# New priority constants and assumed landing times in the planner of a streaming encoder kernel on 8 cores

## What is computed

```
z = x @ w_in                                  # 1024 -> 2560, split in u, v, gb, gc, xin
v = layernorm per head(v);  a = u * (w_s (128x128, masked) @ v + b_s)
b = gb * causal_conv3(gc * xin)
x = LN(ALPHA*x + concat(a, b) @ w_out)
q = x @ w_q; p = softmax(q k^T / 16); x = LN(ALPHA*x + (p v) @ w_mem_o)      # 256 memory tokens
x = LN(ALPHA*x + (silu(x @ w_gate) * (x @ w_up)) @ w_down)                   # 1024 -> 2816 -> 1024
```

## Time and profile before

| | |
|---|---|
| time, median of 3 runs | 3340.69 us (3310.32 to 3353.55) |
| the profiled execution's own time | 3351.93 us |
| its span on the slowest core (core 7) | 3350.4 us |
| spans of the eight cores | 3272.5 to 3350.4 us |
| granted TensorE clock by core | 0.975 to 0.984 |
| DMA | 620.69 MB, mean 185 GB/s |

### The profile page before, as it was taken

The page is one execution under the profiler, slowest core; times in us unless marked ns, Lnnn a source line. Parts: engine busy times, 40 slices in busy tenths (PEclk is TensorE's granted clock), DMA queues, the critical chain, the costliest instruction groups (busy, mean ns, idle before and its releaser), DMA issues.

```text
span 3350.4 us, 54366 instructions; the slowest of 8 cores (3272.5 to 3350.4 us)
## 1 busy us (share of the span) xinstructions
PE 3139.9 (94%) x17604; PEld 1660.0 (50%) x17604; DVE 2181.0 (65%) x4244; ACT 1062.8 (32%) x2012; POOL 383.5 (11%) x356
## 2 busy tenths in 40 slices
PE   8999899999999998899988999799996998979998
PEld 3544444554645454354543545455463553635554
DVE  5774256677767675666756767486683866748664
ACT  4362215242423324133241332323231242323421
POOL 2111011101011000111001011010110101101010
PEclk9999999999999999899998999899998999989999
DMA  9879999675877969767697677956779679786762
GB/s 189 163 160 200 183 258 227 208 193 178 209 179 229 170 209 146 159 214 177 198 149 165 201 189 223 158 178 197 179 229 123 211 188 152 220 135 209 188 181 87
DMA packets 292614, 620.69 MB, mean 185 GB/s; under 512 B 178992, under 2 KB 179120, under 8 KB 262128
## 3 DMA queue, kind: packets, MB, share of 16 engines
q1 hardware_dynamic: 113632, 498.02, 47.8%
q10 hardware_dynamic: 166464, 44.06, 15.5%
q0 software_dynamic: 12240, 75.13, 13.4%
HBM read 582.27 MB, written 64.89 MB: 193 GB/s over the span
## 4 chain that ended last, share of the span: by engine, by line
PE 78%; DMA 17%; issue 2%; DVE 1%; ACT 1%; POOL 0%; ACTq 0%; SPq 0%; DVEq 0%; POOLq 0%
PE bank L91 78%; DMA rb<-wsc 9%; DMA rb<-w_pieces 3%; DMA ra<-wsc 2%; DMA F<-xb 1%; DMA ra<-w_pieces 1%; DMA wsc<-rb 0%; POOL rs L723 0%; DMA xbuf<-x_prompt 0%; DVE rb L659 0%; DMA y_prompt<-xbuf 0%; DVE bank L91 0%; DVE xin L879 0%; DMA WTS<-w_s_t_s 0%; DVE xbuf L754 0%
## 5 line engine op out<-in xcount | busy, mean ns | idle before, releaser
L91 PE MATMUL bank<-F,rb 128*128 128x512 f16 (+2 forms) x5024 | 920.9, 335 | 11.2 <-DMA rb<-wsc 7.5
L91 PE MATMUL bank<-ra,F 128*128 128x512 bf16 x3424 | 797.3, 383 | 29.0 <-DMA ra<-wsc 22.8
L91 PE MATMUL bank<-rb,hT 128*128 128x512 bf16 (+1 forms) x2744 | 639.5, 391 | 110.4 <-DMA rb<-wsc 104.6
L91 PEld LDWEIGHTS bank<-F,rb 128*128 128x128 f16 (+1 forms) x5024 | 489.7, 98 | 372.2 <-issue 15.1
L723 POOL TENSOR_TENSOR rs<-ve,mhalf 128x1 f32<-128x1 f32 (+1 forms) x260 | 334.9, 1291 | 2179.3 <-DVE ve L721 2079.8
L91 PEld LDWEIGHTS bank<-ra,F 128*128 128x128 bf16 x3424 | 335.4, 98 | 399.4 <-issue 43.8
L91 DVE SCALAR_TENSOR_TENSOR xbuf<-xbuf,bank 128x512 f32<-128x512 f32 x384 | 258.6, 678 | 400.5 <-PE bank L91 383.0
L91 PEld LDWEIGHTS bank<-rb,hT 128*128 128x128 bf16 (+1 forms) x2744 | 273.6, 100 | 455.0 <-issue 157.9
L91 PE MATMUL bank<-F,ra 128*128 128x512 bf16 x1920 | 434.2, 382 | 14.2 <-DMA ra<-w_pieces 8.5
L91 PE MATMUL bank<-early,rb 128*128 128x256 f16 (+2 forms) x3104 | 362.1, 262 | 16.3 <-DVE bank L91 9.1
L775 ACT ACTIVATE xb<-xbuf 128x1024 bf16<-128x1024 f32 (+1 forms) x128 | 135.2, 1057 | 630.2 <-DVE mv L749 339.7
(11 more groups left out here) (119 smaller groups left out, 1841.6 us busy)
## 6 DMA issues: line engine op xcount, KB each, us to landing
rb<-wsc SPq DMA_DIRECT2D x455, 512.0 KB, 5.9
ra<-wsc SPq DMA_DIRECT2D x149, 1024.0 KB, 6.0
rb<-w_pieces POOLq DMA_DIRECT2D x34, 1024.0 KB, 14.3
y_prompt<-xbuf SPq DMA_DIRECT2D x60, 512.0 KB, 4.9
xbuf<-x_prompt SPq DMA_DIRECT2D x14, 2048.0 KB, 10.4
wsc<-rb SPq DMA_DIRECT2D x16, 1024.0 KB, 10.5
F<-x_prompt_t POOLq DMA_DIRECT2D x14, 1024.0 KB, 18.6
ra<-w_pieces POOLq DMA_DIRECT2D x13, 1024.0 KB, 17.2
```

Of the source, the lines that this page charges most:

```text
L91: return f(*[r(x) for x in a], **{n: r(x) for n, x in k.items()})
```

## The change

Only constants change. In the planner's table of late landings the transposes go from 10 to 9.0 us, xt from 14 to 12.7, ra loads from 4 to 5.4, and rb loads, which had none, get 3.5. In part A the four combined pieces get one priority, the first output halves change a little, the four attends stand 0.088 apart and not 0.050, and the second output halves get 0.732 and 0.749 and not 0.860 and 0.877, so they rank ahead of all but the first attend. In part B (from tile 1 on) the gate and up pieces are spread over 0.325 and not 0.400, and the down pieces start at 1.494 and not 1.644, each step about as long as before.

```diff
--- before.py
+++ after.py
@@ -135,7 +135,7 @@
 
     LAT = 0.20
     LAT_TO_PE = 0.45
-    LATE = {"tr": 10, "xt": 14, "rA": 4}
+    LATE = {"tr": 9.0, "xt": 12.7, "rA": 5.4, "rB": 3.5}
     DEPTH = 3 << 20
 
     def __init__(self, nc, banks, pools):
@@ -1194,7 +1194,7 @@
             for c in tiles:
                 in_proj_v(c, rg, brg)
             for m in range(4):
-                at(0.183 + 0.001 * m)
+                at(0.183 + 0.000 * m)
                 rg, brg = piece("A", "in_c%d" % m, t)
                 for c in tiles:
                     in_proj_c(c, m, rg, brg)
@@ -1202,18 +1202,18 @@
                 op("sync", lambda e: e.dma_start(out=cvp_o, in_=halo_p[:].rearrange("p m r -> p (m r)")),
                    [buf("halo_p%d" % m) for m in range(4)] + [buf("halo_p")], [], dma="o_cp", nbytes=1 << 12)
             for half in range(2):
-                at(0.480 + 0.086 * half)
+                at(0.483 + 0.070 * half)
                 rg, brg = piece("A", "out%d" % half, t)
                 for c in tiles:
                     out_half(c, half, rg, brg, 0)
             at(0.657)
             pieces = [piece("A", "m%d" % hp, t) for hp in range(2)]
             for s in range(4):
-                at(0.657 + 0.050 * s)
+                at(0.657 + 0.088 * s)
                 for c in tiles:
                     attend(c, s, pieces)
             for half in range(2):
-                at(0.860 + 0.017 * half)
+                at(0.732 + 0.017 * half)
                 for c in tiles:
                     out_half(c, half, *piece("A", "n%d" % half, t), 1)
 
@@ -1326,7 +1326,7 @@
         def run_B(tiles, t):
             n = NF // 2
             for j in range(n):
-                S.prio = t + 1.0 + 0.400 * j / n if t else 0.892 + 0.600 * j / n
+                S.prio = t + 1.0 + 0.325 * j / n if t else 0.892 + 0.600 * j / n
                 if j == 7:
                     pinned.clear()
                 if t == T_SEVEN and j == 0:
@@ -1346,7 +1346,7 @@
                 return
             for half in range(2):
                 for kp in range(3):
-                    S.prio = t + 1.644 + 0.142 * half + 0.081 * kp
+                    S.prio = t + 1.494 + 0.168 * half + 0.083 * kp
                     rg, brg = piece("B", "d%d_%d" % (half, kp), t)
                     for c in tiles:
                         down(c, half, kp, rg, brg)
```

## The result

The changed kernel takes **0.956 of the time before, 95% interval 0.942 to 0.970**: faster. Applied to the median before, that is 0.9561 x 3340.69 = 3194 us. Its own executions are 3171.2 (the profiled one) and 3206.4; two more, in which the cores of one die show a lower granted clock (3343.9 and 3737.7), are left out of every comparison here, as are such executions of the other kernels.

The account below looks back on a forecast made before the run. It took TensorE on core 7, its work plus idle time and the clock lost after it, as the bound. 3350.4 - 157.2 - 24.6 + 63 = 3232 us, 11 less on the median's scale: 3221, stated as 3225, range 3175 to 3325.

Parts of the forecast that it names:

- The bound and the cause: Core 7: TensorE busy 94% of 3350.4 us; a just-started transpose ahead of xt slows all transfers for about 40 us.
- The first rival: Even passes: long flights of xt stay although block 2's transpose starts earlier; 3287 us, no change by the measure, chance 0.25.
- The attends: Part A: wider spacing moves block 2's transpose from 2.1 us ahead of xt to some 8 to 10 in pass 8.
- The sum, core 7: Whole kernel on core 7: 3350.4 - 157.2 - 24.6 + 63 = 3232 us.
- The ten passes: Core 7, passes 4 to 13, each from one xt issue to the next: 187.25 us each, -157.2 in all.
- the tail: Core 7, from the last xt to the end: 398.7 us falls to core 2's undisturbed 374.1, -24.6.
- The +63: Core 7: waits that stay or are new, from loads landing late, VectorE and a long xt, +63 us together.
- Late landings: Loads landing late in the passes: 3 us a pass, times 12, 36 us.
- One long xt: One long flight of xt left on the slowest core: 20 us at most, taken at 15.
- VectorE: After the last attend, FFN layer norms meet other VectorE work: backlog 11.7 us, cost 1 a pass, 12 in all.
- The cover: Around xt: matmuls before first use of loads beside it cover 28.9 or 21.7 us, so a 15.8 us flight everywhere.
- The ring loads in gate-up: Gate-up: rb loads with under 10 us of matmuls between release and first use fall from 46 to 5; waits shrink.

Follow-up runs that it names:

- e12: The kernel before, with attend block 2's DMA transpose held until just behind the transposed-input load (xt) in even passes 4 to 14: 3213.9 and 3217.5 us.
- e5: The changed kernel, with xt and the 1 MB ra load waiting for the VectorE operation that releases block 3's transpose, all leaving within 1 us: 3380.2 us.
- e9: The kernel before with the change's table of late landings alone, all priorities old: ratio 1.003.
- e10: The changed kernel without the new 3.5 us landing of rb loads: ratio 0.970.
- e8: The kernel before with all priorities of the change but the old table of late landings: ratio 0.976.
- e6: The kernel before with only the attends spread 0.088 apart instead of 0.050: ratio 0.965.
- e7: The kernel before with only part B's constants of the change (gate, up and down pieces): 3248.6 us.
- e11: The kernel before with the new table of late landings and the attends 0.088 apart, other priorities old: ratio 0.977.

## Why the prediction was right

It said 3225 us, 3175 to 3325, faster with 0.62; the measurement gives 3194, a ratio of 0.956. Step by step:

*The bound and the cause.* The reading of the earlier trace rows, that a transpose which has just started when xt and a 1 MB piece arrive slows every transfer of the core, was called "my reading and not shown". For xt and the rb loads at its side it is shown now, from both sides: e12 takes the arrangement away in the kernel before, and the long flights and the beat go; e5 puts it into the changed kernel, and the long flights come back. "Every transfer" was too much: the ra load of e5 took 11.9 us where xt took 38.5. The first rival (the order of the two does not matter, 0.25) is refuted by the same runs. It was also where a rule of the Trainium skill led (DMA: Bandwidth & Descriptors, "Queues, rings and completion order": a DMA engine takes its queues in turn). Taking turns may well be what the engines do, but it says nothing about which came first, and in e12 and e5 that is what changes: the instructions and their order on each engine are those of their parents. A little else moves with it: in e12 block 3's transpose goes out 2.8 us later in pass 8, and in e5 xt and the ra load leave some 3 us later, nearer to the transposes behind them. But pass 8 of e5 has none near behind, and xt took 38.5. What in the DMA engines makes the order count stays open.

*The attends.* Block 2's transpose was to move in pass 8 to 8 to 10 us ahead of xt: 9.7. In the other passes it was to be 4 to 6; it is 6.8 to 9.9. Block 3's was to stay "about 7 us behind xt"; it is 2.4 to 3.2. That miss did no harm, and this is luck: the count of the order could not tell it, and e5, with block 3's 0.7 ahead, 3.4 us from there, is slower than before.

*The sum, core 7.* The ten passes were to give -157.2 and gave 1859.7 - 2029.7 = -170.0; the tail -24.6, and 364.9 - 398.7 = -33.8; the stretch up to pass 4, taken as unchanged, +4.4. So the two terms that go were 22 too small: the undisturbed passes of before that I took as the floor, 188.4 and 186.1, still held a little waiting (188.40 with 187.29 busy in the first line of the earlier trace rows). The +63 that were to come back were the mis-sized part. *Late landings*, 3 us a pass, 36 in all: TensorE idles for 0.5 us in ten passes. *One long xt*, 15: there is none in 96. *VectorE*, 12: TensorE's waits for it on the line of the earlier trace rows fell from 9.1 to 3.8 us on the slowest core. Its work in the 50 us from xt is 39.1 us, not 45 to 48, against 33.4 before; that TensorE's eight banks cover what queues up, as the prediction argued, fits this and was not tested. Together -170.0 - 33.8 + 4.4 = -199, and 3350.4 - 199.4 = 3151.0, core 7's span. The slowest core is another one now, at 3169.6, since the cores differ by 19 us after. So for core 7 the sum was 81 too high (3232 against 3151.0). That the forecast of 3225 lies only 31 from 3194 is partly luck: the slowest core is 19 above core 7, and the second execution took 35 more than the profiled one.

*The cover.* The worked-out 28.9 and 21.7 us of matmuls were never needed, as the longest flight is 15.1. Cover without the cure is worth little: e9 had longer leads and 44 long flights, and gained nothing.

*The ring loads in gate-up* got no term of their own, and that was a gap. Their assumed landing is worth nothing with the old priorities and, by the distance of e10 (0.970) from the change (0.956), about 1% with the new; the intervals overlap (0.964 to 0.976, 0.942 to 0.970), so the size is not settled. That the wait it removes is real is seen in e8's timeline.

*The signs to look for.* Passes of 184 to 188 on core 7 (to 189.4 on all), xt of 10 to 15, rb waits of 3.5, a clock of 0.99: all as said or better.

## What to carry to other kernels

If an even-odd beat or a spread between cores shows up in passes of equal instructions, list the long transfers and what was issued in the 3 us ahead of each; a load that leaves while a DMA transpose has just started is the suspect. Let the transpose land first or send it behind, and check this by the issue times of a trace, since counts of matmuls in the planned order misled in four runs here (e6, e7, e9, e11). Follow a wait that is put down to VectorE one step further: at L659 it was a load.

## What the runs showed of the hardware

A DMA transpose is 3.1 us alone. Issued at xt or up to 3.3 us behind it, it takes 11 to 23 us and xt 12 to 16 (the middle 80% of 558 such, medians 15.8 and 13.4). Issued 0.3 to 2.45 us ahead of xt, it takes 4 to 39, median 26, and xt 12 to 36, median 21. What is lost is bandwidth. Two stretches of the kernel before, core 7, in the slow flight and in the next pass's good one, where a transpose is under way too; the last two numbers are the DMA share and GB/s:

```profile
1748.00:1760.00 12.00, 1.79 (x9) 0.59 (x6) 0.00 (x0) 1.06 (x1) 0.00 (x0) 0.68 0.94 40
...
1947.60:1963.40 15.80, 15.80 (x75) 7.15 (x74) 10.14 (x22) 4.36 (x8) 1.15 (x2) 1.00 0.98 237
```

The packets' time is as large a share of the DMA engines' in both (0.94 and 0.98), at 40 GB/s in the one and 237 in the other. The same two places (the second from 1947.5 to 1963) for q10 alone, the queue of ScalarE, which carries the transposes: packets, MB, share of 16 engines. Below them q10 over the whole span, before (core 7) and after (core 2):

```profile
q10 hardware_dynamic: 241, 0.06, 65.0%
...
q10 hardware_dynamic: 144, 0.04, 1.2%
...
q10 hardware_dynamic: 166464, 44.06, 15.5%
...
q10 hardware_dynamic: 166464, 44.06, 9.6%
```

So in the slow flight most of that time belongs to the transposes' small packets, 0.5 us each (12 x 16 x 0.65 / 241) where it is 0.02 in the good one (15.5 x 16 x 0.012 / 144). This says whose packets are long and not why: a packet's time can hold waiting, since the shares of the slow flight's first 21.6 us (1726.4 to 1748) add up to 1.47.

The Trainium skill (Advanced Engine Details and Errata, "X-Bar Transpose (TRN2)") says that transpose DMAs on this chip are as fast as regular ones. With nothing beside it the trace agrees (3.1 us for 256 KB, where an rb load of that size, issued at 1530 us, took 3.2); beside loads a transpose takes up to 15 times as long (48 us). The slow flight is not certain either: of the 350 loads in that place 153 stayed at 20 us or less. Before, cores with the same order differ by it: core 5 (3276.0 us) has 3 long flights of 12, core 7 (3350.4) has 6. The loads around count as well: with the transpose 1.7 to 2.3 us ahead, 32 of 40 flights were long before, and in passes 4, 8 and 12 of e11, at 2.2, only 3 of 24. There, on core 7 in pass 8, no rb load goes out from 7 us ahead of xt to 4 behind, where before three do (6.7 and 5.9 ahead, 0.2 behind). No run separates the two.
